# Two norms between layers by tiles of tokens, split weights kept in V, and modulation rows in other pairs

## The chip, the cores and the metric

The kernel runs on one core of a Trainium2 chip. The metric is the device time of one execution in microseconds. The engines of the core are named as in the profile: PE (TensorE), DVE (VectorE), ACT (ScalarE), POOL (GpSimd) and SP (SyncE); each works through a queue of its own in order, and semaphores join them.

## The reference, cut to what matters

Two blocks in float32 on 256 tokens of width 2048; the second takes the output of the first. Each layer modulates the tokens by rows made from a vector c, projects, attends, gates, projects back and adds to the residual; a norm follows.

```
mod = silu(c) @ w_mod + b_mod; shift, scale, gate = split(mod, 3)
# layer 0 (first block; dilated attention and retention, then RMS norm)
h = rms_norm(x, g) * (1 + scale) + shift
x = rms_norm(x + gate * ((y * silu(z)) @ w_out), final_gain)
# layer 1 (differential attention, then LayerNorm)
h = x * (1 + scale) + shift
x = layer_norm(sqrt(2) * x + gate * ((norm(heads) * silu(g)) @ a_w_out), ln_g, ln_b)
# layer 2 (forgetting attention) takes keys and values from x * (1 + scale_kv) + shift_kv
```

## The kernel before

**Products.** Every float32 matrix is split into a high part (fp32r) and the rest, and a product is three matmuls: high x high (L693), low weights x high (L694), high weights x low (L695). The weights come as steps of two blocks of 128 rows by 512 columns, 0.5 MB each, by SP's queue into 8 slots `raw` (L493). ACT makes the high half `w_hi` in 4 slots (L907), DVE the low half in place, `w_lo` over `raw` (L1221). A step is 12 matmuls on two tiles of 128 tokens, a chunk of 512 columns is 8 steps, a pair is two chunks or 16 steps, and 29 pairs are the whole kernel. `half_used` counts used steps: SP loads a step's slot when the step 8 before is used, ACT splits it when the step 4 before is used. In the listings pair p's step h is (p, h).

**Stages.** Pairs 7 and 8 are the output projection of layer 0, 17 and 18 of layer 1, 27 and 28 of layer 2. Pairs 9 and 19 are the first behind the norm of layers 0 and 1. Attention runs in pairs 4 to 6, 14 to 16 and 24 to 26 at the steps in `STEP_HALVES`: scores of head s, values of head s-3. Heads of retention and of differential attention are normalized: PE writes them (L831), ACT squares them (L1047), POOL makes the root (L573), DVE scales them out of the single bank `o_bank` (`finish_normed`, L1527) at the start of attention step u+4, and the next head's values wait for that.

**Norm and turn.** `add_out` (L1356) takes an accumulated chunk, multiplies by the gate row, adds the residual and takes statistics (L1366, L1371, L1375). `norm` (L1503) then aggregates, waits for POOL's root and normalizes both tiles (L1510, L1512). PE transposes the residual into four banks (L669, eight rounds of four transposes, each round two blocks of channels for both tiles), ACT writes scaled and shifted `act_hi` (L976), DVE computes the same once more into `side` (L1472) and subtracts for `act_lo` (L1477). DVE reaches all that only after it has split the next pair's first four steps.

**Modulation rows.** The products of c with the modulation weights are 176 rows of 1 MB, loaded by POOL's queue into a ring of three (L537) and reduced by DVE (L1236, a multiply with accumulation). `PAIR_TILES` (L64) says how many rows each pair takes and `gemv_steps` (L111) at which steps; layer 1 needs its rows by pair 9, layer 2's keys by pair 19.

**The end.** `last_pair` (L697) does the last four steps of pair 28 first for tile 0, then for tile 1, and `last_out` (L1379) finishes tile 0 under tile 1's products.

## Time and profile before

| | |
|---|---|
| median of 3 runs (lowest, highest) | 1547.94 us (1547.07, 1548.73) |
| profiled execution: time, span | 1544.42 us, 1542.6 us |
| PE busy, share of the span | 1437.7 us, 93% |
| DVE busy | 1182.7 us, 77% |
| ACT busy | 712.2 us, 46% |
| POOL busy | 113.9 us, 7% |
| TensorE clock granted, mean | 0.978 of full |
| moved by DMA | 448.8 MB, mean 291 GB/s |

Busy time is an average over stages. What a stage is bound by is read from its window and from the waits in it. A matmul's shown duration reaches over the next one's start; the distance between starts is what it costs. A pair begins where the last matmul of the pair before ends.

### The profile page before, as it was taken

Reading aid. Unit: us, or ns where it says so; the run is one execution under the profiler, and the core shown is the slowest. Engines: PE = TensorE matmul, PEld = TensorE weight load, DVE = VectorE, ACT = ScalarE, POOL = GpSimd, SP = SyncE. Lnnn points to the kernel's source line nnn. Section 1 sums busy time; section 2 is a strip of 40 time slices with the busy share of each in tenths; the row PEclk is TensorE's granted clock in tenths of the full one; section 3 lists DMA queues with packets and bytes.
Section 4 is the critical chain, followed back from the end, with each engine's and each line's share of the span. In section 5 each row is a group of like instructions: output and inputs, shape, how many; then the busy total and the mean of one; then the engine's idle time right before and its main releaser. Section 6 shows DMA issues by size and latency. Waiting matters only on the chain.

```text
span 1542.6 us, 19099 instructions
## 1 busy us (share of the span) xinstructions
PE 1437.7 (93%) x6634; PEld 1189.8 (77%) x6634; DVE 1182.7 (77%) x1472; ACT 712.2 (46%) x992; POOL 113.9 (7%) x215
## 2 busy tenths in 40 slices
PE   4799999999998799999999989989999999999896
PEld 3677878877777688888887878768888788888785
DVE  6999699577799888788656758898968865655466
ACT  4464554543433344444556643344434544555431
POOL 1111001001001000000000100000000000000000
PEclk9999999999999899999999999989999999999998
DMA  9999899767899599999866658849989676544662
GB/s 389 414 415 412 296 331 373 268 240 270 323 410 398 180 374 364 380 374 359 274 220 194 203 209 341 327 168 374 344 341 340 225 293 219 204 151 137 218 192 95
DMA packets 99868, 448.82 MB, mean 291 GB/s; under 512 B 11424, under 2 KB 13776, under 8 KB 76496
## 3 DMA queue, kind: packets, MB, share of 16 engines
q1 hardware_dynamic: 69840, 249.33, 44.8%
q0 software_dynamic: 26352, 185.63, 30.8%
q10 hardware_dynamic: 3600, 12.85, 2.1%
q8 instruction: 47, 0.77, 0.2%
q14 instruction: 29, 0.24, 0.0%
HBM read 445.65 MB, written 2.12 MB: 290 GB/s over the span
## 4 chain that ended last, share of the span: by engine, by line
PE 75%; DVE 15%; issue 4%; ACT 4%; DMA 2%; DVEq 0%; ACTq 0%; POOL 0%
PE bank L693 19%; PE bank L695 19%; PE bank L694 19%; DVE gw L1236 6%; DVE w_lo L1221 3%; PE bank L655 3%; PE bank L657 3%; PE bank L656 3%; PE bank L831 2%; PE bank L779 2%; DVE w_lo L1228 2%; PE bank L669 1%; DMA raw<-in_t_steps 1%; ACT w_hi L907 1%; PE bank L788 1%
## 5 line engine op out<-in xcount | busy, mean ns | idle before, releaser
L907 ACT CAST w_hi<-raw 128x1024 fp32r<-128x1024 f32 x464 | 485.5, 1051 | 673.1 <-PE bank L695 577.2
L1221 DVE TENSOR_TENSOR w_lo<-raw,w_hi 128x1024 fp32r<-128x1024 f32 x380 | 460.5, 1223 | 263.6 <-ACT w_hi L907 262.5
L693 PE MATMUL bank<-w_hi,act_hi 128*128 128x512 f32 x1536 | 614.8, 400 | 9.0 <-ACT act_hi L976 5.0
L695 PE MATMUL bank<-w_hi,act_lo 128*128 128x512 f32 x1536 | 601.1, 391 | 0.0
L694 PE MATMUL bank<-w_lo,act_hi 128*128 128x512 f32 x1536 | 600.3, 391 | 0.0
L1236 DVE CUSTOM_DVE_ANT_0 gw<-gw,c_act 128x2048 f32<-128x2048 f32 x170 | 388.5, 2286 | 3.5 <-DMA gw<-in_t_ada 3.5
L693 PEld LDWEIGHTS bank<-w_hi,act_hi 128*128 128x128 f32 x1536 | 290.2, 189 | 70.0 <-ACT act_hi L976 5.8
L695 PEld LDWEIGHTS bank<-w_hi,act_lo 128*128 128x128 f32 x1536 | 289.7, 189 | 62.1
L694 PEld LDWEIGHTS bank<-w_lo,act_hi 128*128 128x128 f32 x1536 | 290.3, 189 | 58.3
L1228 DVE TENSOR_TENSOR w_lo<-raw,w_hi 128x1024 fp32r<-128x1024 f32 x84 | 102.2, 1222 | 22.2 <-ACT w_hi L907 22.0
L655 PE MATMUL bank<-w_hi,act_hi 128*128 128x512 f32 x256 | 101.5, 397 | 2.9 <-DVE w_lo L1228 2.9
L537 POOL DMA_DIRECT2D gw<-in_t_mod x96 | 51.1, 532 | 673.7 <-DVE products L1236 667.5
L657 PE MATMUL bank<-w_hi,act_lo 128*128 128x512 f32 x256 | 99.8, 390 | 0.0
L656 PE MATMUL bank<-w_lo,act_hi 128*128 128x512 f32 x256 | 99.7, 389 | 0.0
L655 PEld LDWEIGHTS bank<-w_hi,act_hi 128*128 128x128 f32 x256 | 48.1, 188 | 15.1 <-DVE w_lo L1228 2.9
L657 PEld LDWEIGHTS bank<-w_hi,act_lo 128*128 128x128 f32 x256 | 48.1, 188 | 10.3
L656 PEld LDWEIGHTS bank<-w_lo,act_hi 128*128 128x128 f32 x256 | 48.1, 188 | 9.7
L629 PE MATMUL bank<-w_hi,act_hi 128*128 128x512 f32 x64 | 27.1, 423 | 17.0 <-DVE act_lo L1256 17.0
L1023 ACT ACTIVATE probs<-probs,neg_max 128x128 f32<-128x128 f32 (+1 forms) x80 | 36.6, 458 | 6.6 <-DVE neg_max L1609 6.4
L537 POOL DMA_DIRECT2D gw<-in_t_ada x42 | 22.5, 536 | 220.0 <-DVE products L1236 208.4
L779 PE MATMUL bank<-qk_t 128*128 128x256 f32 (+1 forms) x160 | 37.1, 338 | 0.0
L669 PE MATMUL bank<-ident,resid 128*128 128x128 f32 x96 | 15.2, 319 | 22.1 <-DVE resid L1510 12.0
(151 smaller groups left out, 960.9 us busy)
## 6 DMA issues: line engine op xcount, KB each, us to landing
raw<-in_t_steps SPq DMA_DIRECT2D x464, 512.0 KB, 5.7
gw<-in_t_mod POOLq DMA_DIRECT2D x96, 1024.0 KB, 7.8
gw<-in_t_ada POOLq DMA_DIRECT2D x42, 1024.0 KB, 8.2
gw<-in_t_kv_mod POOLq DMA_DIRECT2D x32, 1024.0 KB, 7.4
area<-in_t_ada POOLq DMA_DIRECT2D x6, 1024.0 KB, 10.9
area<-gate_rows ACTq DMA_DIRECT2D x3, 1024.0 KB, 5.3
area<-in_ln_g ACTq DMA_DIRECT2D x2, 1024.0 KB, 7.2
area<-in_ln_b ACTq DMA_DIRECT2D x2, 1024.0 KB, 10.4
```

Source lines behind the costliest of these rows:

```text
L537: pool.dma_start(dst, src[row + k * P:row + (k + 1) * P].rearrange("p (t n) -> p t n", t=TT)).then_inc(landed, 16)
L655: nc.tensor.matmul(dst, hi, w_hi[:, n % LEAD, k], start=(kt == kt0), stop=False)
L656: nc.tensor.matmul(dst, hi, w_lo[:, n % SLOTS, k], start=False, stop=False)
L657: last = nc.tensor.matmul(dst, lo, w_hi[:, n % LEAD, k], start=False, stop=(kt == kt0 + HALF_KT - 1))
L693: nc.tensor.matmul(dst, hi, w_hi[:, j % LEAD, k], start=(kt == 0), stop=False)
L694: nc.tensor.matmul(dst, hi, w_lo[:, j % SLOTS, k], start=False, stop=False)
L695: return nc.tensor.matmul(dst, lo, w_hi[:, j % LEAD, k], start=False, stop=(kt == KT - 1))
L779: last = nc.tensor.matmul(s_bank[:, c0:c1], q[:, tt * P:(tt + 1) * P], k[:, 0:c1 - c0], start=True, stop=(layer != 2))
L907: nc.scalar.copy(w_hi[:, b], raw[:, j % SLOTS]).then_inc(hi_ready, 1)
L1221: nc.vector.tensor_tensor(w_lo[:, j % SLOTS], raw[:, j % SLOTS], w_hi[:, j % LEAD].bitcast(F32), ALU.subtract).then_inc(lo_ready, 1)
L1228: nc.vector.tensor_tensor(w_lo[:, j % SLOTS], raw[:, j % SLOTS], w_hi[:, j % LEAD].bitcast(F32), ALU.subtract).then_inc(lo_ready, 1)
L1236: nc.vector.tensor_tensor_reduce(out=w, in0=w, in1=c_act[:].rearrange("p (t n) -> p t n", t=TT), scale=1.0, scalar=0.0, op0=ALU.mult, op1= ...
```

## The change

Pairs 8 and 18 run the last four steps first for tile 0 and then for tile 1, as pair 28 does (`tiled_pair`). In these pairs the first four steps of the next pair are split into `early_hi`, which lies over V, so they need no slot of `w_hi`; three are split by DVE before the chain of the norm, the fourth between tile 0's variance and its normalization. DVE's `norm_tiles` gates, adds, measures and normalizes tile 0, then tile 1. A round of the turn is now four blocks of channels of one tile (`TILE_ROUNDS`); six rounds are shifted by DVE, two by ACT, into a buffer of float32 that ACT copies to `act_hi` and DVE subtracts from for `act_lo`. PE's `normed_pair` does the first four steps of the next pair for tile 0, then for tile 1, with the transposes of later rounds between. POOL makes a root for each tile. Layer 0's statistics are sums of squares, three of the four chunks by ACT (`square_chunk`), so DVE takes none in pairs 7 and 8 but the last. `finish_normed` moves from the start of the next attention step to one step after the values (`finish_late`), behind that step's split. Modulation rows move: pairs 2 to 8 take 2, 7, 7, 9, 10, 8, 5 instead of 0, 6, 8, 7, 8, 9, 10, and the rows of pairs 8 and 18 come in steps 1 to 8. The second block's silu of c moves from (5, 7) to (5, 1). ACT's loops over pairs 9, 10 and 19, 20 are written out.

```diff
 
-PAIR_TILES = {3: 6, 4: 8, 5: 7, 6: 8, 7: 9, 8: 10, 9: 7, 10: 7, 11: 7, 12: 7, 13: 7, 14: 3, 15: 3, 16: 3, 17: 4,
+PAIR_TILES = {2: 2, 3: 7, 4: 7, 5: 9, 6: 10, 7: 8, 8: 5, 9: 7, 10: 7, 11: 7, 12: 7, 13: 7, 14: 3, 15: 3, 16: 3, 17: 4,
               18: 5, 19: 7, 20: 7, 21: 7, 22: 6, 23: 5, 24: 4, 25: 4, 26: 3}
 PAIR_STEPS = 2 * STEPS
 
...
+NORM_PAIR = (8, 18)
+TILE_ROUNDS = ((0, 0), (0, 1), (1, 0), (1, 1), (0, 2), (1, 2), (0, 3), (1, 3))
+BY_ACT = (1, 4)
+BY_DVE = (0, 2, 3, 5, 6, 7)
...
-DECAYS_AT, LAMBDA_AT, C_AT = (3, 1), (3, 4), (5, 7)
+SQUARES_AT = {(7, 11): 0, (8, 3): 1, (8, 11): 2}
+DECAYS_AT, LAMBDA_AT, C_AT = (3, 1), (3, 4), (5, 1)
...
-FIRST_PAIR = 3
+FIRST_PAIR = 2
...
-    if pair == 5:
-
-        return [(at, first + i) for i, at in enumerate((0, 2, 9, 10, 12, 13, 15))]
-    return [(1 + i * (13 / n), first + i) for i in range(n)]
+
+    begin, end = {2: (10, 16), 4: (1, 12), 5: (4, 16), 8: (1, 9), 18: (1, 9)}.get(pair, (1, 14))
+    return [(begin + i * ((end - begin) / n), first + i) for i in range(n)]
...
+        with nc.sbuf_tensor("q_and_k", [P, 2, TT, D], F32), \
+                nc.sbuf_tensor("early_hi", [P, LEAD, STEP_KT, CHUNK], F32R) as early_hi:
+            pass
...
+                        pool.wait_ge(var_ready, TT * layer + tt + 1)
...
+            def tile_round(m, i):
+                tt, q = TILE_ROUNDS[i]
+                wait(pe, turned_lo, TURNS * (m - 1) + (i - TURN_BANKS + 1 if i >= TURN_BANKS else 0))
+                for k in range(4):
+                    kt = 4 * q + k
+                    last = nc.tensor.transpose(turn_bank(m, i)[:, k * P:(k + 1) * P],
+                                               resid[:, tt, kt * P:(kt + 1) * P], ident[:])
+                last.then_inc(turned, 1)
+
+            def normed_pair(m, layer):
+
+                p = TURN_PAIR[m]
+                done = TURNS * (m - 1)
+
+                def tile_step(j, tt):
+                    if tt == 0:
+                        pe.wait_ge(lo_ready, PAIR_STEPS * p + j + 1)
+                    for k in range(STEP_KT):
+                        last = tile_products(0, j, k, tt, early_hi[:, j])
+                    return last
+
+                pe.wait_ge(t_free, T["end", layer])
+                pe.wait_ge(normed, TT * layer + 1)
+                tile_round(m, 0)
+                tile_round(m, 1)
+                pe.wait_ge(evacuated, 4 * p - 2)
+                for j in range(LEAD):
+                    pe.wait_ge(turned_hi, done + j // 2 + 1)
+                    pe.wait_ge(turned_lo, done + j // 2 + 1)
+                    tile_step(j, 0)
+                    if j == 2:
+                        pe.wait_ge(normed, TT * layer + 2)
+                        tile_round(m, 2)
+                        tile_round(m, 3)
+                for j in range(LEAD):
+                    pe.wait_ge(turned_hi, done + 2 + j // 2 + 1)
+                    pe.wait_ge(turned_lo, done + 2 + j // 2 + 1)
+                    tile_step(j, 1).then_inc(half_used, 1)
+                    if j in (0, 2):
+                        tile_round(m, 4 + j)
+                        tile_round(m, 5 + j)
+                for h in range(LEAD, PAIR_STEPS):
+                    if h < STEPS:
+                        pe.wait_ge(turned_hi, done + 4 + 2 * (h // 2 - 1))
+                        pe.wait_ge(turned_lo, done + 4 + 2 * (h // 2 - 1))
+                    half(0, p, h // STEPS, h % STEPS)
...
-            pairs(8, 1)
-            pe.wait_ge(normed, TT)
-            turn_and_pair(2, resid, T["end", 0])
+            tiled_pair(8)
+            normed_pair(2, 0)
...
+            def split_early(p, h):
+
+                act.wait_ge(raw_landed[h], 16 * (2 * p + 1))
+                nc.scalar.copy(early_hi[:, h], raw[:, h]).then_inc(hi_ready, 1)
+
+            def square_chunk(n):
+
+                act.wait_ge(summed, TT * (n + 1))
+                for tt in range(TT):
+                    wait(act, chunk_squared, TT * n + tt)
+                    nc.scalar.activation(probs_t[:, 0], resid[:, tt, n * CHUNK:(n + 1) * CHUNK], ACT.Square,
+                                         accum_out=chunk_squares[:, tt, n:n + 1]).then_inc(chunk_squared, 1)
...
+                if i in BY_ACT:
+                    act.wait_ge(turned, TURNS * (m - 1) + i + 1)
+
+                    wait(act, turned_lo, TURNS * (m - 1) + BY_ACT[0] + 1 if i != BY_ACT[0] else TURNS * (m - 1))
+                    full = probs_t[:, 1]
+                    for k in range(4):
+                        kt = 4 * q + k
+                        last = nc.scalar.activation(full[:, k * P:(k + 1) * P], turn_bank(m, i)[:, k * P:(k + 1) * P],
+                                                    ACT.Identity, scale=scales[:, n, kt:kt + 1],
+                                                    bias=shift[:, kt:kt + 1])
+                    last.then_inc(tile_shifted_act, 1)
+                    act.wait_ge(tile_shifted_act, len(BY_ACT) * layer + BY_ACT.index(i) + 1)
+                else:
+                    act.wait_ge(tile_shifted, len(BY_DVE) * layer + BY_DVE.index(i) + 1)
+                    full = side[:, BY_DVE.index(i) % 2]
+                nc.scalar.copy(act_hi[:, 4 * q:4 * q + 4, tt * P:(tt + 1) * P],
+                               full.rearrange("p (k t) -> p k t", k=4)).then_inc(turned_hi, 1)
+
+            def turn_tiles(m, n, shift):
+
+                act.wait_ge(scales_ready, n)
+                def split(j):
+
+                    k = PAIR_STEPS * TURN_PAIR[m] + j
+                    act.wait_ge(raw_landed[j], 16 * (k // SLOTS + 1))
+                    act.wait_ge(half_used, k + 1 - 2 * LEAD)
+                    nc.scalar.copy(w_hi[:, j % LEAD], raw[:, j]).then_inc(hi_ready, 1)
+
+                tile_round(m, n, 0, shift)
+                tile_round(m, n, 1, shift)
+                split(4)
+                split(5)
+                tile_round(m, n, 2, shift)
+                tile_round(m, n, 3, shift)
+                tile_round(m, n, 4, shift)
+                split(6)
+                tile_round(m, n, 5, shift)
+                split(7)
+                tile_round(m, n, 6, shift)
+                tile_round(m, n, 7, shift)
...
+                    if static and p0 in NORM_PAIR and h >= PAIR_STEPS - LEAD:
+                        split_early(p0 + 1, h + LEAD - PAIR_STEPS)
+                    elif static and p0 - 1 in NORM_PAIR and h < LEAD:
+                        pass
...
+                def shift_round(i):
+                    dve.wait_ge(turned, TURNS * (m - 1) + i + 1)
+                    _, q = TILE_ROUNDS[i]
+                    for k in range(4):
+                        kt = 4 * q + k
+                        last = nc.vector.tensor_scalar(side[:, BY_DVE.index(i) % 2, k * P:(k + 1) * P],
+                                                       turn_bank(m, i)[:, k * P:(k + 1) * P], scales[:, n, kt:kt + 1],
+                                                       shift[:, kt:kt + 1], ALU.mult, ALU.add)
+                    last.then_inc(tile_shifted, 1)
...
+                gate_tile(0)
+                sum_tile(0)
+                measure_tile(0)
+                spread_tile(0)
+                split_early(p0 + 1, LEAD - 1)
+                norm_tile(0)
+                gate_tile(1)
+                shift_round(0)
+                sum_tile(1)
+                low_round(0)
+                measure_tile(1)
+                spread_tile(1)
+                low_round(1)
+                norm_tile(1)
+                chunk = 2 * p0 + 2
+                chunk_halves(0, 2, chunk, (4,))
+                whole_round(2)
+                whole_round(3)
+                whole_round(4)
+                whole_round(5)
+                chunk_halves(0, 2, chunk, (5, 6))
+                whole_round(6)
+                whole_round(7)
+                chunk_halves(0, 2, chunk, (7,))
...
+            def finish_late(p, h):
+
+                step = steps_of(*divmod(PAIR_STEPS * p + h - 1, PAIR_STEPS))
+                if step:
+                    layer, u = step[0], step[1] - 3
+                    if 0 <= u < UNITS[layer] and is_normed(layer, u):
+                        finish_normed(layer, u)
...
-                if 0 <= s - 4 < units and is_normed(layer, s - 4):
-                    finish_normed(layer, s - 4)
...
-            pair(8, add_out(0))
-            norm(0)
-            turn_scaled(2, 1, mod[:, A_SHIFT], A_SCALE)
+            pair(8, to_norm(0, 2, 1, mod[:, A_SHIFT], A_SCALE))
```

## Rows read from the trace of the kernel before

**Rows 1.** Windows: start:end, length, busy of PE, PEld, DVE, ACT, POOL, clock, DMA.
```profile
177.00:221.30 44.30, 43.85 (x193) 35.66 (x191) 39.82 (x58) 25.47 (x30) 3.17 (x6) 1.00 0.85 300
...
274.30:338.90 64.60, 62.84 (x326) 52.97 (x325) 43.11 (x68) 32.99 (x53) 5.15 (x10) 1.00 0.71 253
...
338.90:397.50 58.60, 52.04 (x221) 41.95 (x219) 44.93 (x47) 23.01 (x33) 7.76 (x15) 0.97 0.77 295
...
451.20:499.10 47.90, 45.40 (x193) 36.82 (x191) 47.90 (x49) 16.86 (x16) 5.29 (x10) 0.96 1.00 401
...
499.10:561.70 62.60, 50.17 (x225) 41.78 (x226) 56.77 (x72) 25.14 (x34) 4.98 (x9) 0.89 0.70 269
...
605.20:648.80 43.60, 43.60 (x194) 36.12 (x193) 34.63 (x31) 18.84 (x21) 4.23 (x8) 1.00 0.96 365
...
998.90:1058.90 60.00, 49.14 (x225) 41.04 (x226) 54.08 (x68) 25.14 (x34) 4.45 (x8) 0.91 0.65 246
...
345.00:349.00 4.00, 3.35 (x9) 2.71 (x10) 2.23 (x4) 0.18 (x1) 0.00 (x0) 0.66 0.75 269
```

**Rows 2.** Waits of PE: who waited for whom, total us, times, longest.
```profile
PE bank L669 <- DVE area L1353: 12.7, 3, 4.5
...
PE bank L669 <- DVE resid L1510: 12.0, 1, 12.0
...
PE bank L669 <- DVE resid L1512: 10.1, 1, 10.1
...
PE bank L831 <- DVE area L1537: 6.6, 3, 3.1
...
PE bank L693 <- DVE w_lo L1221: 4.0, 4, 2.5
```

**Rows 3.** Timeline at the end of pair 8: start, length, instruction, idle before.
```profile
499.78 3.49 DVE L1221 TENSOR_TENSOR w_lo<-raw,w_hi 128x1024 fp32r<-128x1024 f32 x3
...
503.18 1.28 DVE L1366 TENSOR_TENSOR side<-bank,area 128x512 f32<-128x512 f32 x2
...
515.21 0.77 PE L693 MATMUL bank<-w_hi,act_hi 128*128 128x512 f32 x1 [0.49 <-ACT act_hi L976]
...
515.77 0.63 PE L694 MATMUL bank<-w_lo,act_hi 128*128 128x512 f32 x1
...
516.20 0.63 PE L695 MATMUL bank<-w_hi,act_lo 128*128 128x512 f32 x1
```

**Rows 4.** Timeline at the end of pair 18.
```profile
1006.31 2.60 DVE L1512 TENSOR_SCALAR resid<-resid,moments,rstd 128x2048 f32<-128x2048 f32 x2 [0.84 <-POOL rstd L573]
...
1013.13 0.47 PE L693 MATMUL bank<-w_hi,act_hi 128*128 128x512 f32 x1 [0.79 <-ACT act_hi L976]
...
1015.98 1.04 PE L669 MATMUL bank<-ident,resid 128*128 128x128 f32 x8
```

**Rows 5.** Timelines of DVE and POOL, at pair 18's end and in pair 28.
```profile
1005.56 0.71 POOL L573 TENSOR_TENSOR rstd<-mean_sq,minus_half 128x2 f32<-128x2 f32 x1 [12.06 <-DVE mean_sq L1501]
...
1524.37 0.69 DVE L1392 TENSOR_TENSOR side<-bank,area 128x512 f32<-128x512 f32 x1 [3.08 <-PE bank L695]
...
1527.08 1.54 POOL L568 TENSOR_TENSOR rstd<-mean_sq,minus_half 128x1 f32<-128x1 f32 x1 [107.71 <-DVE mean_sq L1401]
```

**Rows 6.** The weight loads of L493, all 464, from issue to landing.
```profile
DMA to landing us min/median/max: 3.3/5.7/19.7
```

**Rows 7.** Groups by line and form: total us, mean ns of one, idle before.
```profile
L907 ACT CAST w_hi<-raw 128x1024 fp32r<-128x1024 f32 x464 | 485.5, 1051 | 673.1 <-PE bank L695 577.2 <-DMA raw<-in_t_steps 46.9 <-PE bank L657 42.9
...
L1236 DVE CUSTOM_DVE_ANT_0 gw<-gw,c_act 128x2048 f32<-128x2048 f32 x170 | 388.5, 2286 | 3.5 <-DMA gw<-in_t_ada 3.5
...
L964 ACT CAST act_hi<-bank 128x512 fp32r<-128x512 f32 x24 | 13.4, 588 | 25.4 <-PE bank L669 25.4
...
L1570 DVE TENSOR_SCALAR area<-bank,rden 128x128 f32<-128x128 f32 x48 | 14.5, 344 | 0.0
```

More of the change, by code:

```diff
@@ L225, in two_blocks @@
         ROOTS += [("head", layer, u) for u in range(UNITS[layer]) if is_normed(layer, u)]
-        ROOTS.append(("norm", layer))
+        ROOTS += [("norm", layer, tt) for tt in range(TT)]
     HEAD_ROOTS = {key: n for n, key in enumerate(k for k in ROOTS if k[0] == "head")}
@@ L880, in _ @@
             turn_and_pair(3, area[:, Q], T["end", 1])
-            pairs(18, 1)
-            pe.wait_ge(normed, 2 * TT)
-            turn_and_pair(4, resid, T["end", 1])
+            tiled_pair(18)
+            normed_pair(4, 1)
             pairs(20, 2)
@@ L947, in pair @@
                         scores_step(*step)
[L948 removed]
+                    if static and p0 in NORM_PAIR and h >= PAIR_STEPS - LEAD:
+                        split_early(p0 + 1, h + LEAD - PAIR_STEPS)
+                    elif static and p0 - 1 in NORM_PAIR and h < LEAD:
+                        pass
+                    elif not (last and h >= PAIR_STEPS - LEAD):
                         chunk_halves(i, 2, 2 * p0 + (h + LEAD) // STEPS, [(h + LEAD) % STEPS])
@@ L1445, in turn_scaled, with scale_turn @@
             def turn_scaled(m, n, shift, scale):
+                shift = scale_turn(n, shift, scale)
+                for r in range(TURNS):
+                    turn_round(m, n, r, shift)
+            def scale_turn(n, shift, scale):
                 gain = {0: VEC_GAIN, 1: VEC_FINAL, 2: VEC_LN_G}.get(n)
@@ L1463, in turn_scaled @@
                 dve.wait_ge(scales_ready, n)
-                for r in range(TURNS):
-                    turn_round(m, n, r, shift)
+                return shift
             def turn_round(m, n, r, shift):
@@ L1503, in norm, with square_most @@
-            def norm(layer):
-                measure(layer)
-                dve.wait_ge(root_ready, ROOTS[("norm", layer)] + 1)
-                for tt in range(TT):
-                    x, r = resid[:, tt], rstd[:, tt:tt + 1]
+            def square_most():
+                dve.wait_ge(chunk_squared, 3 * TT)
+                link(nc.vector.tensor_tensor(most_squares[:], chunk_squares[:, :, 0], chunk_squares[:, :, 1], ALU.add))
+                link(nc.vector.tensor_tensor(most_squares[:], most_squares[:], chunk_squares[:, :, 2], ALU.add))
+                link(nc.vector.tensor_scalar(most_squares[:], most_squares[:], 1.0 / D, NORM_EPS, ALU.mult, ALU.add))
@@ new lines, in norm_tiles, with gate_tile, sum_tile, measure_tile @@
+            def norm_tiles(layer, m, n, shift, scale):
+                p0 = NORM_PAIR[layer]
+                cols = slice(D - CHUNK, D)
+                x = resid[:, :, cols]
+                steps = PAIR_STEPS * (p0 + 1)
+                if layer == 0:
+                    square_most()
+                shift = scale_turn(n, shift, scale)
+                dve.wait_ge(gate_landed, 16 * (layer + 1))
+                def gate_tile(tt):
+                    if tt == 0:
+                        dve.wait_ge(tile_done, layer + 1)
+                    else:
+                        dve.wait_ge(half_used, steps)
+                    nc.vector.tensor_tensor(side[:, tt], acc_banks[2 + tt][:], area[:, K, 0, cols], ALU.mult
+                                            ).then_inc(evacuated, 1)
+                def sum_tile(tt):
+                    dve.wait_ge(evacuated, 4 * p0 + 2 + tt + 1)
+                    nc.vector.scalar_tensor_tensor(out=x[:, tt], in0=x[:, tt], scalar=DN_ALPHA if layer else 1.0,
+                                                   in1=side[:, tt], op0=ALU.mult, op1=ALU.add).then_inc(summed, 1)
+                def measure_tile(tt):
+                    dve.wait_ge(summed, 8 * layer + 6 + tt + 1)
@@ new lines, in norm_tiles, with to_norm, take @@
+                spread_tile(1)
[11 more added lines that the diff above has]
+                chunk_halves(0, 2, chunk, (7,))
+            def to_norm(layer, m, n, shift, scale):
+                def take(i, p0, c):
+                    if c == 0:
+                        add_out(layer)(i, p0, c)
+                    else:
+                        norm_tiles(layer, m, n, shift, scale)
+                return take
```

116 lines of the change are left out of this document (80 added, 36 removed).

## The prediction

> **What bounds the kernel now.** I read the windows by pair first. TensorE is the engine that must never stop: a pair of weight chunks without attention takes it 43.5 us (the clean pair 11 of [rows 1], whose window is rounded up to 43.6), or 2.72 us for each of its 16 steps of 12 products, and there VectorE is busy only 34.6 us of it. So a pair's price is 43.5 us, its transposes, its attention work and its stalls. The waits of TensorE [rows 2] then name the stalls: 12.0 and 10.1 us for the two norms between the layers (L1510, L1512), 12.7 us for the three starts behind a gated layer (L1353), 6.6 us for a head's output that VectorE has not normalized yet (L1537), 4.0 us for low halves of weights (L1221). The change touches all but L1353. Last I read the timeline around the two norms [rows 3, 4] for what stands between the last product of a pair and the first of the next.
>
> Call T the end of pair 8 (499.1 us) or of pair 18 (998.9 us). Pair 9 takes 62.6 us and pair 19 60.0 us [rows 1]. Of that 43.5 is products and 32 transposes are 4.1, four times the 1.04 us that eight take at the full clock [rows 4]. Left over are 15.0 and 12.4 us: waits of 12.5 and 10.9 [rows 2 to 4], and 2.5 and 1.5 of a fallen clock.
>
> **Part 1, the last four steps by tiles of tokens.** Tile 0's 24 products now end 24 x 0.227 = 5.4 us before T. No product is added. VectorE's chain for one tile is measured in the last pair, which works like this already: gating begins at 1524.37 and POOL's root at 1527.08, so 2.6 us for gating, adding, measuring and variance and 0.1 to hand over [rows 5]. When is VectorE free for it? The load of the next pair's step j is issued when step 8+j of this pair is used, at T-19.0, T-16.3 and T-13.6 for the first three, and lands 5.7 us later in the median [rows 6]. ScalarE, which splits step 15 at T-9.8 and then these three at 1.05 us each [rows 7], and VectorE behind it at 1.14 (3.49 us for three [rows 3]), end them near T-4.4. Scales and shifts (and layer 0's small sums) take 0.6. So the chain runs from T-3.7 to T-1.1 (layer 0: 0.7 later, for ScalarE's squares delay it by 1.5).
>
> **Part 2, the early split into V.** Three of four low halves leave the path: at the first boundary VectorE still did three of them between the last product and the gating, which began only at 503.18, T+4.1 [rows 3]. The fourth is queued ahead of tile 0's normalization, 1.22 us, while POOL makes the root: T+0.15. The root itself: 0.71 us on two columns with VectorE idle, 1.54 us on one column beside a VectorE operation with two inputs in SBUF [rows 5]. The fourth split is such an operation, so I take the long one: the root is there about 0.5 us behind the split. Then 1.34 us for one tile (two in 2.60 [rows 4]). TensorE starts to transpose at T+2.0 (layer 0: T+2.6) instead of T+10.1 and T+12.0.
>
> The Trainium skill has a rule that speaks against this place for the split: its page GPSIMD Engine Reference, section Key points, says that GpSimd shares its SBUF interfaces with VectorE and contends with instructions that have two SBUF inputs. By that rule the root waits for the split; without it the sum below would be 1.0 us better over both boundaries. The 1.54 against 0.71 us of the trace agrees, though the two also differ in columns.
>
> **Part 3, the turn by tiles.** Per boundary eight rounds of four transposes, six shifted by VectorE (four instructions of 128x128) and two by ScalarE. Four at 0.34 us each [rows 7], overlapping by 0.08, are 1.1 us; ScalarE's copy of 128x512 is 0.59 [rows 7], the subtraction 0.69 as any two-input operation of that size [rows 5]. First products: T+2.0, 0.6 for round 0, 1.1, 0.6, 0.7 and four handovers of 0.05 make T+5.2, where they began at T+14.3 (1013.13 [rows 4]) and T+16.1 (515.21 [rows 3]). But products now need VectorE soon after. Its queue from T to step 8 of the next pair holds: two normalizations 2.7, tile 1's chain 2.5, six shifts 6.7, eight subtractions 5.5, five splits 6.0, two modulation rows at 2.29 [rows 7], 4.5: 27.9 us of work, about 33 with its own waits for ScalarE's copy inside each round (0.7 us x 6). TensorE's to the same point is 4.1 + 8 x 2.72 = 25.9. Followed round by round, TensorE waits 0.8 us at tile 1's first product (shift, copy and subtraction of round 2 stand behind the second normalization and a split), 1.9 at step 6 (rounds 6 and 7 stand behind two splits), 1.3 at step 8 and 0.6 at step 9 (the two rows are queued ahead of their splits). In all 2.0 + 2.2 + 4.6 = 8.8 us of waits in layer 1, 9.4 in layer 0, and I add 0.8 for a clock that falls for a short while. Saved: 12.4 - 9.6 = **2.8 us** and 15.0 - 10.2 = **4.8 us**. The later waits have no row; their bounds are 0 (VectorE keeps up, as now) and 4.6 more (each round also pays one handover more and the clock stays down for the first tile), so 0 to 7 and 0 to 9.
>
> **Part 4, rows moved.** Pairs 7 and 8 lose one and five modulation rows. In pair 8 VectorE is busy 47.9 of 47.9 us [rows 1]; five rows fewer are 11 us, layer 0's statistics (now squares on ScalarE) 1.3 more, so it is far from binding and the pair takes 43.5: **4.4 us**. In pair 7 the two small waits for low halves, 0.6, go: **0.6 us**. The rows go to pairs 2 (two), 3 (one), 5 (two) and 6 (two); pair 4 loses one. In pair 5 VectorE has 43.1 of 64.6 us busy; it hides two. Silu of c moves from step 7 to step 1 of pair 5 and pays up to two table loads more on ScalarE, hidden while TensorE has four steps of split weights in hand. In pair 3 VectorE is already 39.8 of 44.3 busy; one row more makes 42.1 of 43.5. I charge **-0.5 us** for pairs 2 to 5, with bounds of -3 and +1.
>
> **Part 5, heads finished one step after their values.** Pair 6 takes 58.6 us, of which 6.6 are the waits for L1537 and, at a clock granted at 0.66 for 4 us [rows 1], 1.5 or so the slow products after them: 8.1 to be had. The finish of a head now stands one step earlier, behind that step's split. That split ends 1.05 + 1.14 after the step is used, the finish some 0.9 later (two of 128x256, where two of 128x128 take 0.6), at 3.1 against the 2.72 at which TensorE wants the bank: 0.4 us left, twice. Two rows more come at a spacing of 1.3 steps: VectorE then needs 1.3 x 1.14 + 2.21 = 3.7 us (a row of 2.29 hands over 0.08 before its end) for what TensorE does in 3.5, and the DMA 1.05 MB in 3.5 us and 0.52 in 2.7, 490 GB/s where pair 8 reached 401 with its engines at 1.00 [rows 1]. The first steps of pair 6, with attention in them, and three rows in the ring carry most of it; I charge 1.3. Saved: 8.1 - 0.8 - 1.3 = **6.0 us**, bounds 1 and 8. In layer 1 TensorE never waits for L1537: nothing. ScalarE's unrolled loops and POOL's root per tile: nothing beyond what is counted.
>
> **Sum.** 2.8 + 4.8 + 4.4 + 0.6 - 0.5 + 6.0 = 18.1 us. The profiled execution took 1544.4 (span 1542.6); it would take 1526.3, span 1524.5. The median of the runs lies 3.5 above it, 1547.94, so I forecast **1529.8 us**.
>
> **Rivals.**
> 1. Density moves with the rows. Pair 6 becomes what pair 8 is now: VectorE without a gap, DMA at its ceiling, low halves late. For it: ten rows in one pair is the spacing that cost pair 8 its 4.4 us, and pair 3 is near full. Against: pair 6 has three steps of attention that give VectorE time, and no sums to add. Pair 6 then saves 2, pairs 2 to 5 cost 2.5: 12.1 saved, 1535.8 us.
> 2. VectorE keeps up behind the norms (its waits inside a round overlap better than I count): 3 to 4 us more at each boundary, 1522.5 us.
> 3. The change doesn't do what it says, as the early loads are late: landings reach 19.7 us [rows 6]. The fourth split, ahead of the normalization, then holds it up: a load that lands 11 us after T-10.9 delays both boundaries by 2 to 3 us each: 1535 us.
> 4. Slower: the clock. The waits are shorter but more: T to T+22 has five, with tiny bursts of transposes between. If the granted clock is down at 0.5 from the first transposes to the end of tile 1's products, 48 products cost 0.43 instead of 0.23 us and 32 transposes 0.25 instead of 0.13, 13.4 us per boundary less some 3.5 of waits that this fills, some 20 in both: 1549.8 us. It decides when the clock doesn't come back before the 48 products are over. Spacing at the low clock is that of 515.77 to 516.20 [rows 3]. Against: after 12 us of idling the first products had the long durations of 0.77 and 0.63 only a few times [rows 3], after 10 us the first one was already at 0.47 [rows 4].
>
> **How the numbers follow.** My forecast 0.62 (its own range 1525 to 1535); rival 1 0.16, rival 2 0.11, rival 3 0.06, rival 4 0.03, something untold near no change 0.02. The range, with bounds of the later waits and of pair 6, is 1520 to 1540. About 0.2% is what a measurement of this kernel can tell from none. Faster 0.95, same 0.02, slower 0.03.
>
> **What would show it.** In the changed trace: tile 0's gating starts 3 to 5 us before the pair's last product ends (part 1); the first transpose comes 2 to 3 us after it, POOL's root lies over 1 us long beside the split (part 2); waits of TensorE of about 2.2, 0.8, 1.9 and 1.3 us in pair 9 and the same in pair 19, pairs of 57 to 58 us (part 3); pair 8 at 43.5 us (part 4); pair 6 at 52 to 53 us, waits for the finished head under 1 us (part 5). I am wrong if pair 9 or 19 has a wait above 4 us, if pair 6 stays above 55, or if pairs 2 to 5 grow by over 3 us.

## The result and the profile after

| | before | after |
|---|---|---|
| median of 5 runs (lowest, highest) | 1548.73 us (1547.07, 1550.06) | 1541.15 us (1536.59, 1542.33) |
| profiled execution: time, span | 1544.42, 1542.6 us | 1536.59, 1534.8 us |
| TensorE clock granted, mean | 0.978 | 0.982 |

The ratio is 0.9945, 95% interval 0.9927 to 0.9962: faster by 7.6 us, where 18.1 were forecast, and 1.15 us above the upper end of the range.

Windows by pair of the changed kernel (3, 5, 6, 8, 9, 19), in the columns of [rows 1], and at last three short windows at the first norm:

```profile
178.80:224.20 45.40, 44.14 (x194) 35.89 (x193) 41.29 (x59) 25.16 (x30) 3.21 (x7) 1.00 0.89 328
277.30:342.50 65.20, 62.78 (x325) 52.90 (x324) 49.31 (x72) 35.76 (x55) 4.24 (x8) 1.00 0.72 253
342.50:395.70 53.20, 50.45 (x221) 40.79 (x219) 45.67 (x51) 23.02 (x33) 11.58 (x19) 1.00 0.88 339
448.80:492.40 43.60, 43.52 (x192) 35.69 (x191) 39.24 (x46) 20.39 (x25) 3.46 (x6) 1.00 0.89 348
492.30:552.40 60.10, 50.80 (x226) 40.58 (x226) 50.69 (x69) 24.04 (x33) 5.05 (x9) 0.94 0.64 242
...
990.90:1051.10 60.20, 51.12 (x226) 40.82 (x226) 51.22 (x69) 24.03 (x33) 5.17 (x9) 0.94 0.66 245
...
492.30:494.50 2.20, 0.04 (x2) 0.05 (x1) 1.74 (x3) 0.00 (x0) 0.75 (x1) 1.00 0.82 290
494.50:498.20 3.70, 1.13 (x8) 0.83 (x9) 3.39 (x8) 1.60 (x5) 0.00 (x0) 0.61 0.48 175
498.20:502.00 3.80, 3.80 (x9) 3.03 (x10) 3.21 (x6) 2.94 (x5) 0.56 (x1) 0.50 0.00 0
```

Pair 8 fell from 47.9 to 43.5 us and pair 6 from 58.6 to 53.1, as predicted. Pair 9 fell by 2.6 only and pair 19 not at all: 60.2 for the 60.0 of [rows 1]. The last three rows say why to look at the clock. It is granted at 1.00 in the first wait, falls in the stretch of the eight transposes and the second wait (0.61 on average), and from 498.2 to 502.0, in the first products of the pair, it is at 0.50, the lower of its two levels (1.2 of 2.4 GHz).

Waits of TensorE, as in [rows 2]:

```profile
PE bank L711 <- DVE act_lo L1715: 7.0, 4, 2.6
PE bank L735 <- issue: 4.5, 2, 2.4
...
PE bank L711 <- ACT act_hi L1035: 3.7, 2, 1.9
...
PE bank L711 <- DVE w_lo L1350: 3.6, 5, 1.1
PE bank L896 <- DVE area L1786: 2.6, 3, 1.6
```

L735 (the first transposes behind a normalization), L1715 and L1035 (a turned round) and most of L1350 (low halves) are what became of the 12.0 and 10.1 us: 9.3 us in pair 9, 9.1 in pair 19. L896 is the wait for a finished head, 6.6 us before. TensorE around the end of pair 8 (T = 492.3); an entry gives start, length, instruction, and in brackets the idle time before:

```profile
494.48 1.16 PE L735 MATMUL bank<-ident,resid 128*128 128x128 f32 x8 [2.16 <-issue]
498.20 0.77 PE L711 MATMUL bank<-early_hi,act_hi 128*128 128x512 f32 x1 [2.57 <-DVE act_lo L1715]
498.77 0.63 PE L712 MATMUL bank<-w_lo,act_hi 128*128 128x512 f32 x1
499.19 0.63 PE L713 MATMUL bank<-early_hi,act_lo 128*128 128x512 f32 x1
...
502.17 0.39 PE L711 MATMUL bank<-early_hi,act_hi 128*128 128x512 f32 x1
```

The first product comes at T+5.9 (predicted 5.8 for this layer). But nine products fill the 3.97 us from 498.20 to 502.17, where nine at 0.227 are 2.04. VectorE and POOL in the same place:

```profile
489.14 0.69 DVE L1657 TENSOR_TENSOR side<-bank,area 128x512 f32<-128x512 f32 x1
...
491.40 1.22 DVE L1355 TENSOR_TENSOR w_lo<-raw,early_hi 128x1024 fp32r<-128x1024 f32 x1
493.09 1.29 DVE L1692 TENSOR_SCALAR resid<-resid,rstd 128x2048 f32<-128x2048 f32 x1 [0.47 <-POOL rstd L587]
```

```profile
491.57 1.48 POOL L587 TENSOR_TENSOR rstd<-mean_sq,minus_half 128x1 f32<-128x1 f32 x1 [15.58 <-DVE mean_sq L1679]
498.83 0.56 POOL L587 TENSOR_TENSOR rstd<-mean_sq,minus_half 128x1 f32<-128x1 f32 x1 [5.78 <-DVE mean_sq L1679]
```

Gating starts at T-3.2, and the normalization waits 0.47 us for a root that lies 1.48 us beside the fourth split. The chain runs as it was worked out. What failed is the price of the gaps it leaves.

### The profile page after: what moved, and what is told of

It reads as the page before. It is cut to its first block, busy times and chain, and to the rows that moved or that the text cites. A ratio compares the mean times of both kernels' runs of the same rounds, so it can differ in the third digit from the quotient of the medians.

```text
span 1534.8 us, 19093 instructions
## 1 busy us (share of the span) xinstructions
PE 1440.1 (94%) x6634; PEld 1189.0 (77%) x6634; DVE 1180.3 (77%) x1486; ACT 718.7 (47%) x1006; POOL 118.8 (8%) x217
## 4 chain that ended last, share of the span: by engine, by line
PE 75%; DVE 14%; issue 4%; ACT 4%; DMA 2%; POOL 0%; DVEq 0%; ACTq 0%
PE bank L711 20%; PE bank L713 20%; PE bank L712 20%; DVE gw L1370 5%; PE bank L672 2%; PE bank L674 2%; PE bank L673 2%; DVE w_lo L1350 2%; PE bank L896 2%; PE bank L844 2%; DVE w_lo L1362 2%; DMA raw<-in_t_steps 1%; PE bank L686 1%; PE bank L853 1%; DVE side L1702 1%
## 5 line engine op out<-in xcount | busy, mean ns | idle before, releaser
L970 ACT CAST w_hi<-raw 128x1024 fp32r<-128x1024 f32 x448 | 468.8, 1050 | 654.3 <-PE bank L713 553.3
L1350 DVE TENSOR_TENSOR w_lo<-raw,w_hi 128x1024 fp32r<-128x1024 f32 x372 | 450.1, 1222 | 247.0 <-ACT w_hi L970 245.8
L711 PE MATMUL bank<-w_hi,act_hi 128*128 128x512 f32 x1504 | 600.8, 399 | 11.6 <-ACT act_hi L1035 3.7
L713 PE MATMUL bank<-w_hi,act_lo 128*128 128x512 f32 x1504 | 587.8, 391 | 0.0
L711 PEld LDWEIGHTS bank<-w_hi,act_hi 128*128 128x128 f32 x1504 | 283.5, 188 | 72.2 <-ACT act_hi L1035 4.5
L713 PEld LDWEIGHTS bank<-w_hi,act_lo 128*128 128x128 f32 x1504 | 283.0, 188 | 60.5
L1362 DVE TENSOR_TENSOR w_lo<-raw,w_hi 128x1024 fp32r<-128x1024 f32 x84 | 101.8, 1219 | 20.6 <-ACT w_hi L970 20.2
L672 PE MATMUL bank<-w_hi,act_hi 128*128 128x512 f32 x256 | 101.6, 397 | 3.9 <-DVE w_lo L1362 3.9
L674 PE MATMUL bank<-w_hi,act_lo 128*128 128x512 f32 x256 | 99.8, 390 | 0.0
L672 PEld LDWEIGHTS bank<-w_hi,act_hi 128*128 128x128 f32 x256 | 48.1, 188 | 16.4 <-DVE w_lo L1362 6.0
L674 PEld LDWEIGHTS bank<-w_hi,act_lo 128*128 128x128 f32 x256 | 48.0, 188 | 10.3
L646 PE MATMUL bank<-w_hi,act_hi 128*128 128x512 f32 x64 | 27.7, 433 | 16.1 <-DVE act_lo L1390 15.9
L555 POOL DMA_DIRECT2D gw<-in_t_kv_mod x32 | 17.4, 544 | 226.4 <-DVE products L1370 219.7
```

The source lines that it names most:

```text
L555: pool.dma_start(dst, src[row + k * P:row + (k + 1) * P].rearrange("p (t n) -> p t n", t=TT)).then_inc(landed, 16)
L672: nc.tensor.matmul(dst, hi, w_hi[:, n % LEAD, k], start=(kt == kt0), stop=False)
L674: last = nc.tensor.matmul(dst, lo, w_hi[:, n % LEAD, k], start=False, stop=(kt == kt0 + HALF_KT - 1))
L711: nc.tensor.matmul(dst, hi, w[:, k], start=(kt == 0), stop=False)
L713: return nc.tensor.matmul(dst, lo, w[:, k], start=False, stop=(kt == KT - 1))
L970: nc.scalar.copy(w_hi[:, b], raw[:, j % SLOTS]).then_inc(hi_ready, 1)
```

## The experiments

The length of a pair, in us, in each profiled execution (the last matmul of a pair to that of the next; a clean pair is 43.5):

| | 3 | 5 | 6 | 7 | 8 | 9 | 15 | 19 |
|---|---|---|---|---|---|---|---|---|
| before | 44.2 | 64.6 | 58.6 | 53.7 | 47.8 | 62.7 | 60.0 | 60.0 |
| after | 45.4 | 65.2 | 53.1 | 53.2 | 43.5 | 60.1 | 61.5 | 60.2 |
| e1, the same again | 45.4 | 66.8 | 53.0 | 53.2 | 43.5 | 60.7 | 61.7 | 60.3 |
| e2, long fill | 45.4 | 66.9 | 53.1 | 53.3 | 43.5 | 59.9 | 61.6 | 60.0 |
| e3, before + rows | 45.4 | 66.9 | 57.8 | 52.9 | 43.5 | 60.0 | 60.1 | 60.0 |
| e4, after, old norms | 45.4 | 65.3 | 53.0 | 56.4 | 43.5 | 60.1 | 61.7 | 60.0 |
| e5, after, old finish | 45.4 | 66.9 | 57.9 | 52.9 | 43.5 | 60.1 | 61.6 | 60.2 |
| e6, short fill | 45.4 | 65.2 | 53.1 | 53.4 | 43.5 | 58.3 | 60.1 | 58.5 |
| e7, split later | 45.4 | 66.9 | 53.0 | 54.6 | 43.5 | 60.3 | 60.1 | 60.3 |
| e8, e4 + fill | 45.4 | 65.2 | 53.0 | 53.3 | 43.5 | 59.6 | 61.7 | 59.5 |
| e9, e6 + other rows | 44.2 | 66.8 | 53.1 | 55.3 | 43.5 | 57.5 | 61.7 | 59.0 |

Pair 15, and pair 5 behind the moved rows, take one of two lengths some 1.6 us apart, with the same waits in them. Pair 7 is longest in e4, e9 and e7, by its first wait (6.8, 5.2 and 5.8 us for 4.3 in the changed kernel): there VectorE waited 1.9, 0.3 and 1.4 us for the load of a modulation row at the end of pair 6, which now has ten. In the others it didn't. That is rival 1 of the prediction, in some executions only.

**e1: the changed kernel again**, unedited, for its spread and beside the others on one chip.

> The changed kernel once more, nothing edited: a second trace of it and five more runs. Theory A (the clock behind the two norms took the missing gain): pairs 9 and 19 are again 60 us long, with 9.1 to 9.3 us of waits and a granted clock near 0.5 for 5 to 6 us behind each norm; the dips of the first trace in pair 0 (0.72 for 6 us) and pair 15 (0.89 for 15 us) lie elsewhere or are absent, as the change has no part in them. Rival B (those two dips belong to the change, by the rows moved or the finish moved): they stand in the same places again, 1.7 and 1.5 us. Time by both: 1538 to 1542 us.

1539.92 us (1537.34 to 1543.02) beside 1548.31 of before; ratio 0.9951 (0.9934 to 0.9969). The gain of about 8 us is real, and so is the shortfall. Of the two other falls of the clock that the expectation asks about, the one in pair 0 was absent (86.6 us, 88.2 in the first profile) and the one in pair 15 stood there again.

**e2: products that keep TensorE busy in both gaps.** Eight products of constants into a bank not in use, before the wait for tile 0 and behind its transposes.

```diff
+            def fill(n):
+                for _ in range(n):
+                    nc.tensor.matmul(banks[6][:, 0:SEQ], ident[:], neg_upto[:], start=True, stop=True)
...
+                fill(8)
                 pe.wait_ge(normed, TT * layer + 1)
                 tile_round(m, 0)
                 tile_round(m, 1)
+                fill(8)
```

> The changed kernel with TensorE kept at work in the two gaps behind each norm: eight matmuls of 128x256 on constants before the wait for tile 0's norm and eight behind the first two rounds of transposes, all into a bank that the next rounds overwrite. Nothing else. Theory A: the granted clock stays at 1.00 behind both norms, pairs 9 and 19 take 57.5 us instead of 60.1 and 60.2 and the time falls by 5 to 6 us against the changed kernel, to about 1535. Rival B (the clock there costs little, VectorE is what sets the pair's length): the later waits grow by what the clock gives back, pairs 9 and 19 stay at 59 to 60 us and the time within 1.5 us of the changed kernel. If the sixteen matmuls overrun the gaps, both pairs get longer by the overrun, up to 1 us.

```profile
494.78 3.61 PE L742 MATMUL bank<-neg_upto,ident 128*128 128x256 f32 x16
498.23 1.04 PE L735 MATMUL bank<-ident,resid 128*128 128x128 f32 x8
499.10 3.62 PE L742 MATMUL bank<-neg_upto,ident 128*128 128x256 f32 x16
502.37 0.58 PE L711 MATMUL bank<-early_hi,act_hi 128*128 128x512 f32 x1
```

TensorE's timeline shows each product as two, 0.43 us for both: eight overran a gap of 2.2 us, and the first product came at T+7.4 (T = 494.9). 1537.6 us, ratio 0.9933 (0.9917 to 0.9949): not to be told from e1, and inconclusive by its own mistake. e6 repeats it with a fill that fits.

**e3: the kernel before with the rows moved alone** (part 4).

```diff
-PAIR_TILES = {3: 6, 4: 8, 5: 7, 6: 8, 7: 9, 8: 10, 9: 7, 10: 7, 11: 7, 12: 7, 13: 7, 14: 3, 15: 3, 16: 3, 17: 4,
+PAIR_TILES = {2: 2, 3: 7, 4: 7, 5: 9, 6: 10, 7: 8, 8: 5, 9: 7, 10: 7, 11: 7, 12: 7, 13: 7, 14: 3, 15: 3, 16: 3, 17: 4,
...
-DECAYS_AT, LAMBDA_AT, C_AT = (3, 1), (3, 4), (5, 7)
+DECAYS_AT, LAMBDA_AT, C_AT = (3, 1), (3, 4), (5, 1)
...
```

> The kernel before with the rows moved alone (rows by pair, their steps, silu of c at step 1 of pair 5); norms and the finish of heads as before. Theory A: pair 8 falls from 47.8 to 43.5 us and pair 7 by 0.5, pair 3 grows by 1 and pair 5 by 0.5, pair 6 by 0 to 1 (ten rows, with the waits for the finished head still there): 1546 us, 3 us faster than before. Rival B (the rows moved are what costs the missing gain): pairs 2 to 6 grow by as much as pairs 7 and 8 shrink, 1548 to 1550.

1542.41 us (theory A had 1546), ratio 0.9971 (0.9958 to 0.9985). Pair 8 gives its 4.3 us. The surprise is pair 9: 60.0 instead of 62.7 with the old norm. VectorE's timeline at its start (T = 498.85):

```profile
500.01 1.23 DVE L1220 TENSOR_TENSOR w_lo<-raw,w_hi 128x1024 fp32r<-128x1024 f32 x1 [1.49 <-ACT w_hi L906]
501.16 1.28 DVE L1365 TENSOR_TENSOR side<-bank,area 128x512 f32<-128x512 f32 x2
```

Gating starts at T+2.3, where in [rows 3] three splits stood ahead of it and it started at T+4.1. The three were the backlog of pair 8's modulation rows. Moving rows removes them without any work on the norm: 1.5 us of waits less, and 1.1 less of a low clock.

**e4: the changed kernel with the norms of before** (parts 4 and 5 without 1 to 3): e3 and, in VectorE's program, the late finish of part 5 (called in two places, the first is shown):

```diff
+                    finish_late(p, h)
                     for at, g in gemv_steps(p):
...
-                if 0 <= s - 4 < units and is_normed(layer, s - 4):
-                    finish_normed(layer, s - 4)
```

> The changed kernel with both norms as before (no tiles of tokens, no early split into V, whole rounds of the turn), rows and the finish of heads as changed. Its distance to the changed kernel is what the whole work on the norms is worth. Theory A: that is 2.6 us in pair 9 and nothing in pair 19, so 1544 us, 2 to 3 above the changed kernel. My forecast had 7.6 for it: then it would be 1549. Rival B (the forecast of 7.6 holds and the gain was lost elsewhere): 1547 to 1549.

1537.18 us (1536.39 to 1538.22), ratio 0.9931 (0.9911 to 0.995): not slower than the changed kernel itself, and pairs 9 and 19 take 60.1 and 60.0 us where the tiles give 60.1 and 60.2. So **the whole work on the norms brings nothing** at the clocks that these runs had. TensorE's timeline behind T = 494.1:

```profile
504.28 3.67 PE L668 MATMUL bank<-ident,resid 128*128 128x128 f32 x16 [10.17 <-DVE resid L1511]
508.44 0.47 PE L692 MATMUL bank<-w_hi,act_hi 128*128 128x512 f32 x1 [0.48 <-ACT act_hi L975]
508.74 0.39 PE L693 MATMUL bank<-w_lo,act_hi 128*128 128x512 f32 x1
```

The clock is low here too, but only in the sixteen transposes: the products behind them have their short durations at once (0.39 in place of 0.63).

**e5: the changed kernel with the heads finished one step earlier, as before**: the two calls of `finish_late` out, and `finish_normed(layer, s - 4)` back in the attention step.

```diff
-                    finish_late(p, h)
...
+                if 0 <= s - 4 < units and is_normed(layer, s - 4):
+                    finish_normed(layer, s - 4)
```

> The changed kernel with the finish of heads put back to the start of the next attention step; all else as changed. Theory A (the late finish gains in pair 6 and costs in pair 15 through the clock): pair 6 grows from 53.0 to 58 us, pair 15 shrinks from 61.6 to 60.0, the granted clock there is 1.00 throughout: 3 us slower than the changed kernel, 1543. Rival B (pair 15's dip is chance): pair 15 stays at 61.6 in this trace too, 1545.

1543.56 us, ratio 0.9979 (0.9962 to 0.9995). The wait for the head in the list of waits, 2.6 us in the changed kernel:

```profile
PE bank L896 <- DVE area L1784: 7.4, 3, 2.8
```

Pair 6 takes 57.9 us for 53.1: part 5 is worth 4.8 us. Pair 15 takes its longer length here as well, so the late finish is not what makes it.

**e6: the fill of e2 cut to fit**: `fill(4)` and `fill(5)` in place of 8 and 8.

> As e2_warm, but with four and five filling matmuls instead of eight and eight: in e2_warm one took 0.43 us, not 0.22, and they overran both gaps. Now they end inside the gaps. Theory A (the fallen clock eats the gain behind the norms): first products 5.8 us after the end of pair 8 as in the changed kernel, clock 1.00, pairs 9 and 19 take 57.5 us, 5 us less in all: 1535. Rival B (VectorE's queue sets the length of these pairs, so that the products' earlier end only lengthens the later waits): pairs 9 and 19 take 59 to 60 us, 1538 to 1540.

```profile
495.72 1.09 PE L735 MATMUL bank<-ident,resid 128*128 128x128 f32 x8 [0.39 <-DVE resid L1699]
496.65 2.32 PE L742 MATMUL bank<-neg_upto,ident 128*128 128x256 f32 x10
499.47 0.47 PE L711 MATMUL bank<-early_hi,act_hi 128*128 128x512 f32 x1 [0.50 <-DVE act_lo L1722]
499.78 0.40 PE L712 MATMUL bank<-w_lo,act_hi 128*128 128x512 f32 x1
```

The first product starts at T+5.9 (T = 493.6), at the same distance as without fill, and the products behind it are shown with 0.39 to 0.40 us instead of 0.63. Pairs 9 and 19 take 58.3 and 58.5 us: 1.8 and 1.7 less for work that computes nothing, and just what the nine slow products cost (3.97 - 2.04 = 1.9). That lies between theory A's 57.5 and rival B's 59. In pair 19 the clock fell all the same, but later, from 1019.1 to 1022.5, behind the wait of 1.88 us at step 6. It cost nothing there: the two waits for low halves that stand behind it in pair 9 (1.02 and 0.26 us) are absent in pair 19, and from the first product on both pairs take 52.4 us. 1532.97 us (1531.55 to 1540.0), ratio 0.9918 (0.9893 to 0.9943). That is about 7 us below e1, which ran on another chip; the two pairs explain 3.5 to 4.2 of it, and where the rest lies is not shown. The nearer measure is e7 below, on the same chip, with pairs 9 and 19 as long as in the changed kernel: 1535.6 us, 2.6 above e6, with intervals that overlap.

**e7: the fourth early split moved behind tile 1's variance**, to take the disputed neighbour from POOL's root.

```diff
                 spread_tile(0)
-                split_early(p0 + 1, LEAD - 1)
                 norm_tile(0)
...
                 spread_tile(1)
+                split_early(p0 + 1, LEAD - 1)
                 low_round(1)
```

> The changed kernel with the fourth early split taken from between tile 0's variance and its normalization and put behind tile 1's variance. Theory A (POOL's root waits for the interface that the split holds): the root takes 0.56 us there as it does for tile 1, not 1.48; tile 0 is normalized 0.9 us earlier and so is the first transpose; the pairs shorten by 0.5 to 1 us each, 1538. Rival B (a root on one column takes 1.5 us by itself when POOL has been idle): 1.48 us stays, normalization starts 0.5 earlier only by the split that is gone.

```profile
493.82 0.57 POOL L587 TENSOR_TENSOR rstd<-mean_sq,minus_half 128x1 f32<-128x1 f32 x1 [15.27 <-DVE mean_sq L1679]
500.31 1.47 POOL L587 TENSOR_TENSOR rstd<-mean_sq,minus_half 128x1 f32<-128x1 f32 x1 [5.93 <-DVE mean_sq L1679]
```

POOL's rows for tile 0 and tile 1: the long root moves with the split. 1535.6 us, ratio 0.9932 (0.9909 to 0.9955), but the pairs stay at 60.3 us. At the first norm the raw weights landed later in this run (ScalarE waited 0.6 and 0.8 us for two of them) and gating began at T-1.9. At the second the first product came at T+5.8 instead of T+6.2, but ten products ran at the low clock behind it instead of eight, and from there to the end the pair took 54.5 us instead of 54.0. What the root gives back went into the clock.

**e8: the fill in the kernel with the old norms** (e4 with `fill(21)` ahead of its wait for the norm): what is tiling worth when the clock is out of the way?

> e4_norms_before (both norms as before, rows and finish of heads as changed) with 21 filling matmuls in each 10 us gap ahead of the norm, 9.1 us of work. Theory A: with the clock up the transposes cost 2.1 instead of 3.5 us in the first four rounds and the first products run full speed: pairs 9 and 19 at 58.3 instead of 60.0, 3.5 us less than e4: 1534. Against e6_warm_fit it tells what the tiles of tokens are worth once the clock is out of it: by theory A 1.5 us over both norms, by my forecast 7.6. Rival B: no change against e4.

```profile
502.07 1.97 PE L668 MATMUL bank<-ident,resid 128*128 128x128 f32 x16 [1.11 <-DVE resid L1518]
505.78 0.47 PE L692 MATMUL bank<-w_hi,act_hi 128*128 128x512 f32 x1 [1.74 <-ACT act_hi L982]
```

1534.67 us, ratio 0.9918 (0.9891 to 0.9946). The transposes take 1.97 us instead of 3.67, but the wait for ScalarE's high halves behind them grows from 0.48 to 1.74: pairs 9 and 19 shorten by only 0.5. So in the old norms most of the low clock was hidden under the shift, and with a full clock the tiles are worth 59.6 - 58.3 = 1.3 and 59.5 - 58.5 = 1.0 us.

**e9: e6 with other rows**: pair 3 back at six, and the seven rows of pairs 9 and 19 spaced from step 5 to 15 instead of 1 to 14.

```diff
-PAIR_TILES = {2: 2, 3: 7, 4: 7, 5: 9, 6: 10, 7: 8, 8: 5, 9: 7, 10: 7, 11: 7, 12: 7, 13: 7, 14: 3, 15: 3, 16: 3, 17: 4,
+PAIR_TILES = {2: 2, 3: 6, 4: 8, 5: 9, 6: 10, 7: 8, 8: 5, 9: 7, 10: 7, 11: 7, 12: 7, 13: 7, 14: 3, 15: 3, 16: 3, 17: 4,
...
-    begin, end = {2: (10, 16), 4: (1, 12), 5: (4, 16), 8: (1, 9), 18: (1, 9)}.get(pair, (1, 14))
+    begin, end = {2: (10, 16), 4: (1, 12), 5: (4, 16), 8: (1, 9), 18: (1, 9), 9: (5, 15), 19: (5, 15)}.get(pair, (1, 14))
```

> The changed kernel with 4 + 5 filler products in the two gaps behind each norm (as in e6), and two moves of modulation rows: pair 3 has six rows and pair 4 eight, as in the kernel before, and in pairs 9 and 19 the seven rows are spaced from step 5 to step 15 instead of from step 1 to step 14. The output is the same. Theory A (the prediction's part 3: the waits at steps 8 and 9 of pairs 9 and 19, 1.02 and 0.26 us, come from two rows queued ahead of the low halves; and the 1.2 us of pair 3 come from its seventh row): both waits go, the wait of 1.88 us ahead of step 6 (two rounds behind two splits) stays or grows by at most one row not yet there; pairs 9 and 19 at 56.8 to 57.3 us against 58.3 and 58.5 in e6, pair 3 at 44.2 us against 45.4; in all 3.8 us less than e6, some 1529 us. Rival B (VectorE is behind as a whole after the second normalization; the rows only stand where the backlog shows): the waits move to steps 10 to 15 where the rows now are closer together, pairs 9 and 19 stay at 58 us or more, and the time is 1532 us. Rival C: pair 3 keeps its 45.4 us, as its wait comes from the two rows of pair 2 or from the layer's start, and not from the seventh row.

1532.19 us (1529.25 to 1536.82), ratio 0.9907 (0.989 to 0.9923); against e6 no difference that can be measured. Pair 3 is back at 44.2: its 1.2 us belong to the seventh row (rival C is out). The waits at steps 8 and 9 of pair 9 are gone, as theory A has it, but half of rival B came too: pair 20 grew from 44.8 to 46.8. Pair 19 is 1.6 us longer than pair 9. The clock fell at step 6, as in e6, and now no wait stands behind to take it up; eight products have the long distances:

```profile
1020.54 0.47 PE L711 MATMUL bank<-w_hi,act_hi 128*128 128x512 f32 x1 [1.85 <-ACT act_hi L1042]
...
1021.22 0.63 PE L713 MATMUL bank<-w_hi,act_lo 128*128 128x512 f32 x1
1021.64 0.63 PE L711 MATMUL bank<-w_hi,act_hi 128*128 128x512 f32 x1
...
1024.95 0.39 PE L711 MATMUL bank<-w_hi,act_hi 128*128 128x512 f32 x1
```

So the same fall of the clock cost nothing in e6 and 1.6 us here. And ahead of the first norm one of the three early splits waited for its weights:

```profile
490.21 1.22 DVE L1362 TENSOR_TENSOR w_lo<-raw,early_hi 128x1024 fp32r<-128x1024 f32 x1 [0.87 <-ACT early_hi L1013]
```

ScalarE, which makes the high half first, had waited 1.05 us for the load. Gating began at T-2.1 instead of T-3.2 and the first gap kept 1.45 us of wait; at the second norm it kept 1.47, behind a load for which ScalarE had waited 2.4 us. The program of pairs 5 to 8 is that of e6, where no split ahead of the first norm waited for a load, so this 1 us belongs to the timing of the loads (rival 3 of the prediction, in small).

## Why the prediction was wrong, point by point

**What was right.** Part 1: gating starts at T-3.2 (predicted T-3.0 in layer 0). Part 2: the root lies 1.48 us beside the split, and the first transposes start 2.2 us after T (predicted 2.6). Part 3, the waits: 2.16, 2.57, 1.12, 0.25, 1.86, 1.06 and 0.28 us in pair 9, in all 9.3 (predicted 9.4), and 9.1 in pair 19 (predicted 8.8). One term in it was too small and is hidden by another: the four shifts of a round take 1.37 us for the 1.1 predicted, and the first transposes came 0.4 us earlier than predicted. Part 4: pair 8 at 43.5. Part 5: pair 6 saved 5.5 us (predicted 6.0). Pair 7: 0.5 (0.6).

**The step that failed first: "I add 0.8 for a clock that falls for a short while".** Pair 9 is 43.5 of products, 4.2 of transposes, 9.3 of waits, and 3.1 more; pair 19 has 3.4 more. e6 splits this. From the first product to the end of pair 9 it takes 52.4 us at the full clock: 43.5 of products, 3.1 of the other 24 transposes, 4.5 of waits and 1.3 of starts behind those waits, which the sum took as free (a product costs 0.227 us but is shown 0.39 long, so a wait counted from its end misses 0.16, and the product behind a wait costs 0.31). The changed kernel takes 54.2 us for the same stretch with 4.6 of waits: 1.8 more, the clock. In pair 19 the clock cost 1.6, with eight slow products, and 0.5 more in the first transposes, 1.57 us for eight where e6 has 1.10. The sum held 0.8 for the clock, which took 1.8 and 2.1, and nothing for the starts. The shortfall is 2.3 us in pair 9 and 3.0 in pair 19 (of it 0.3 of waits).

The mistake in the reasoning is where a low clock falls. I read in [rows 3, 4] that the first product behind 10 us of idling was nearly at full speed, and took that as evidence that short gaps are milder still. e4 and e8 show what stood in between: sixteen transposes in a row ran at the low clock, and their time was hidden under the shift by VectorE and ScalarE. The turn by tiles puts only eight transposes there, about 1.1 us, with a second wait of 2.57 us behind them. In pair 9 the clock fell only near the end of these transposes (at 495.3) and came back at 502.2, so the products carry the low clock. Rival 4 named this mechanism, with 48 slow products; there were nine and eight, and the chance of 0.03 went to its extreme instead of to its middle.

**The second: pair 9 was compared with the wrong counterfactual.** Its 15.0 us of stall held 2.7 that e3 takes away by moving rows alone: VectorE's three late splits were the backlog of pair 8. I gave the removal to part 2, and in the sum that is no error (it was counted once). But what parts 1 to 3 could bring on top of part 4 was then never 7.6 us. By my own figures it was 4.9, and after the clock and the starts it is nothing: 60.1 and 60.2 us against 60.1 and 60.0 in e4.

**The third: -0.5 us for pairs 2 to 5.** They cost 1.8: pair 3 grew by 1.2, in every kernel with seven rows there and in none with six, and pair 5 by 0.7. VectorE was 39.8 of 44.3 us busy in pair 3 [rows 1]; full on average was not far enough from late. The profile of the changed kernel was a mild one: in the ten executions with rows moved these four pairs took 1.2 to 4.3 us more than before, in five of them over the 3 that the prediction called a sign of being wrong. Pair 5 took its long length in six, and pair 2 took 46.4 to 49.4 us for 47.1.

**What no part is shown to cause: 3.3 us.** Pairs 0 and 15 were 1.8 and 1.5 us longer in the profiled execution of the changed kernel. Pair 15 has the same waits in both lengths (2.2 and 0.6 us); in the long one the clock falls at the end of the first. Its window in after, and that of the same pair in e6:

```profile
776.80:838.30 61.50, 58.71 (x280) 48.72 (x279) 38.95 (x78) 34.95 (x73) 4.51 (x9) 0.97 0.59 197
806.10:812.10 6.00, 5.95 (x23) 5.15 (x24) 1.85 (x6) 3.07 (x5) 0.00 (x0) 0.73 0.41 160
```

```profile
773.30:833.40 60.10, 57.30 (x280) 47.50 (x279) 40.48 (x84) 34.49 (x77) 5.43 (x11) 1.00 0.63 206
```

It happened with and without parts 1 to 3 and part 5; the rows of part 4 are moved in all of these kernels. Of the ten profiled executions of the changed kernel and the experiments seven have the long pair 15; of the kernel before there is one profile, with the short one, so whether the change makes it likelier stays open.

**The account**, in the profiled executions: 5.3 us short at the two norms, 1.3 in pairs 2 to 5, 0.5 in pair 6, 0.2 in pairs 7 and 8, 3.3 in pairs 0 and 15: 10.6, where 10.3 lie between 1536.59 and the 1526.3 of the sum (the rest is rounding and small gains in other pairs). The forecast of the median missed by 1.1 more: the prediction put it 3.5 us above the profiled execution, and it lay 4.6 above. On which side of the range's 1540 the median falls is luck: e1, the same kernel, has 1539.92. That 7.6 to 8.4 us came where 18.1 were forecast is not.

**The rule of the Trainium skill** weighed in part 2 (page GPSIMD Engine Reference, section Key points: GpSimd contends with VectorE instructions that have two SBUF inputs) holds in this kernel: with tile and column count the same, the root takes 0.57 us alone and 1.47 beside the split (e7), so the columns were not what set 0.71 and 1.54 apart in [rows 5].

**The best kernel** of these by its ratio is the changed one with the short fill: e6 at 0.9918 of before, e9 at 0.9907, where the changed kernel stands at 0.9945. The interval of e9 (up to 0.9923) lies clear of the changed kernel's (from 0.9927), that of e6 overlaps with it. e8, the old norms with a fill, stands at 0.9918 as well; only the lengths of pairs 9 and 19 tell it from e6.
